# First projection of a two-block transformer kernel: another order of key evictions, pool sums, value-chunk splits and the first query-chunk split

## The reference, cut to what matters

```python
h_x = _modulate(x, g_pre_mix[l], sh1, sc1)      # 256 tokens
h_c = _modulate(ctx, g_pre_mix[l], csh1, csc1)  # 256 context tokens
u_x, q_x, k_x, v_x = _project(h_x, w_in[l])     # 4 x 512 columns
u_c, q_c, k_c, v_c = _project(h_c, w_in[l])     # only k_c and v_c are used
attn_x = _neighbourhood_attention(q_x, k_x, v_x, k_c, v_c, rpb[l])
mix_x = concat([_pool_mixer(u_x, pool_w[l], pool_scale[l]), attn_x]) @ w_out[l]
```

## Time and profile before

| | |
|---|---|
| median of 3 runs | 928.18 us (926.5 to 929.54) |
| profiled execution, its own time | 929.46 us |
| its span in the trace | 927.5 us |
| mean granted TensorE clock | 0.968 of full |
| PE busy | 863.7 us, 93% of the span |
| DVE busy | 521.0 us, 56% |
| ACT busy | 444.2 us, 48% |
| POOL busy | 44.6 us, 5% |
| DMA | 165.87 MB, mean 179 GB/s |

### The profile page before, as it was taken

The page is one execution under the profiler, slowest core; times in us unless marked ns, Lnnn a source line. Parts: engine busy times, 40 slices in busy tenths (PEclk is TensorE's granted clock), DMA queues, the critical chain, the costliest instruction groups (busy, mean ns, idle before and its releaser), DMA issues.

```text
span 927.5 us, 13973 instructions
## 1 busy us (share of the span) xinstructions
PE 863.7 (93%) x5434; PEld 734.9 (79%) x5434; DVE 521.0 (56%) x904; ACT 444.2 (48%) x797; POOL 44.6 (5%) x55
## 2 busy tenths in 40 slices
PE   5898899979999999899999999898798899999996
PEld 3696655749999998679999999785465699999995
DVE  2344167476776565665555554677445565555554
ACT  3553045265545444554444444765445554444442
POOL 1000000000000000000000000055100000000000
PEclk9999799979999999999999999998779999999998
DMA  8966338425787565356555554564012265555521
GB/s 325 397 250 248 116 136 319 159 90 163 262 280 226 182 186 172 102 173 231 182 184 182 196 185 146 207 215 158 0 46 69 92 207 179 194 191 181 185 92 46
DMA packets 45105, 165.87 MB, mean 179 GB/s; under 512 B 4976, under 2 KB 5104, under 8 KB 44784
## 3 DMA queue, kind: packets, MB, share of 16 engines
q1 hardware_dynamic: 45040, 164.98, 51.7%
HBM read 163.91 MB, written 1.05 MB: 178 GB/s over the span
## 4 chain that ended last, share of the span: by engine, by line
PE 83%; DVE 5%; ACT 4%; issue 4%; DMA 2%; POOL 1%; SPq 0%; ACTq 0%; DVEq 0%; POOLq 0%
PE ps L1361 13%; PE ps L1363 13%; PE ps L1362 12%; PE ps L1381 12%; PE ps L1383 12%; PE ps L1385 12%; DMA raw<-in_w_mod_p 2%; PE ps L1608 2%; PE ps L1407 1%; ACT hi L449 1%; DVE lo L866 1%; ACT PT L461 1%; PE ps L1795 1%; PE ps L1801 1%; PE ps L1592 1%
## 5 line engine op out<-in xcount | busy, mean ns | idle before, releaser
L866 DVE TENSOR_TENSOR lo<-raw,hi 128x1024 fp32r<-128x1024 f32 (+1 forms) x247 | 298.9, 1218 | 180.2 <-ACT hi L449 180.0
L449 ACT ACTIVATE hi<-raw 128x1024 fp32r<-128x1024 f32 (+1 forms) x247 | 257.1, 1049 | 78.3 <-PE ps L1385 59.9
L1361 PE MATMUL ps<-Th,hi 128*128 128x256 f32 (+1 forms) x960 | 276.1, 288 | 3.1 <-DVE lo L866 1.7
L1363 PE MATMUL ps<-Th,lo 128*128 128x256 f32 (+1 forms) x960 | 275.0, 287 | 0.0
L1362 PE MATMUL ps<-Tl,hi 128*128 128x256 f32 (+1 forms) x960 | 275.0, 287 | 0.0
L1381 PE MATMUL ps<-hi,Th 128*128 128x512 f32 (+2 forms) x524 | 180.6, 404 | 13.9 <-issue 7.0
L1361 PEld LDWEIGHTS ps<-Th,hi 128*128 128x128 f32 x960 | 184.0, 192 | 8.5 <-issue 3.0
L1362 PEld LDWEIGHTS ps<-Tl,hi 128*128 128x128 f32 x960 | 183.9, 192 | 3.7
L1363 PEld LDWEIGHTS ps<-Th,lo 128*128 128x128 f32 x960 | 183.8, 191 | 1.3
L1383 PE MATMUL ps<-lo,Th 128*128 128x512 f32 (+2 forms) x524 | 175.7, 394 | 0.0
L1385 PE MATMUL ps<-hi,Tl 128*128 128x512 f32 (+2 forms) x524 | 175.4, 394 | 0.0
(11 more groups left out here) (189 smaller groups left out, 622.4 us busy)
## 6 DMA issues: line engine op xcount, KB each, us to landing
raw<-in_ffn_down SPq DMA_DIRECT2D x44, 512.0 KB, 3.6
raw<-in_w_mod_p SPq DMA_DIRECT2D x40, 512.0 KB, 6.1
raw<-in_ffn_gate SPq DMA_DIRECT2D x40, 512.0 KB, 3.2
raw<-in_ffn_up SPq DMA_DIRECT2D x40, 512.0 KB, 3.2
raw<-in_w_mlp_out SPq DMA_DIRECT2D x32, 512.0 KB, 4.5
raw<-in_w_mlp_in SPq DMA_DIRECT2D x28, 512.0 KB, 4.4
raw<-in_w_out SPq DMA_DIRECT2D x16, 512.0 KB, 5.6
raw<-in_w_in_q SPq DMA_DIRECT2D x8, 512.0 KB, 5.7
```

The costliest lines, as they stand in the source:

```text
L449: e.activation(hi[h % RING][:, 0:w], raw[n % RAW][:, 0:w], ACT.Copy).then_inc(s_hi, 1)
L866: e.tensor_tensor(lo[h % RING][:, 0:w], raw[n % RAW][:, 0:w], hi[h % RING][:, 0:w], ALU.subtract).then_inc(s_lo, 1)
L1361: e.matmul(o, a, Th[:, k, c0:c1], start=(k == 0), stop=False)
L1363: return e.matmul(o, b, Th[:, k, c0:c1], start=False, stop=(k == KT - 1))
```

## The change

Three edits, on ACT and DVE alone. The instructions are the same in number and kind; only their order differs. PE, SP and POOL are as before.

1. The split of q0 (`split(4)`) stands ahead of the context's norm on both engines.
2. On ACT, the splits of v0 and v1 stand behind the evictions of k2 and k3, those of v2 and v3 behind `mod_part(0)`. k0 and k1 are evicted right after the split of k3.
3. On DVE, `window(0)` to `window(2)` stand ahead of `lo` of k3 and `window(3)` behind it; then come `lo` of v0 and v1, `mod_part(0)`, and `lo` of v2 and v3.

```diff
@@ ScalarE
                 first_turned(0, j)
+            split(4)
             first_norm(2)
             first_norm(3)
-            split(4)
@@
-            split(CH["w_in_q", 3] + RING)
+            split(CH["w_in_k", 3])
             for a in range(4):
                 h = CH["w_in_k", a]
                 e.wait_ge(s_used, h + 1)
                 e.activation(kT[:, a, 0:512], ps[ROT[a]][:, :], ACT.Copy).then_inc(s_k, 1)
                 e.activation(kT[:, a, 512:672], ps[ROT[a]][:, 0:160], ACT.Copy).then_inc(s_k, 1)
-                split(min(h + RING, CH["w_in_v", 3]))
+                if a >= 2:
+                    split(CH["w_in_v", a - 2])
             mod_part(0)
+            split(CH["w_in_v", 3])
             load_table(ACT.Exp)
@@ VectorE
                 first_low(0, j)
+            split(4)
             first_sum(2)
             first_sum(3)
             first_scaled(2)
             first_scaled(3)
-            split(4)
@@
-            split(CH["w_in_q", 3] + RING)
+            split(CH["w_in_k", 2])
@@
-            for a in range(4):
-                window(a)
-                split(min(CH["w_in_k", a] + RING, CH["w_in_v", 3]))
+            for g in range(3):
+                window(g)
+            split(CH["w_in_k", 3])
+            window(3)
+            split(CH["w_in_v", 1])
             mod_part(0)
+            split(CH["w_in_v", 3])
```

## The result

| | before | changed |
|---|---|---|
| median | 927.51 us (4 runs, 926.5 to 929.54) | 913.58 us (4 runs, 910.07 to 917.61) |
| ratio | | 0.9852, 95% interval 0.9824 to 0.988 |
| profiled execution, its span | 929.46, 927.5 | 917.61, 915.7 |
| mean granted clock in it | 0.968 | 0.973 |

The change is 13.9 us faster where I forecast 11.3; 913.58 lies 0.4 us under the low end of my range, so the range was wrong. (The kernel before has one run more than when I forecast, hence 927.51 and not 928.18.) The interval of the ratio means a gain of 11.1 to 16.3 us and holds the forecast one, so the first question is whether anything is missing from the sum at all.

What follows compares the result with a forecast made beforehand. PE bounds the kernel, losing time only where it stands still or runs slowly, held up by ACT's and DVE's order. 6.96 + 2.37 + 0.35 + 1.66 = 11.34 us takes 928.18 to 916.9; 8-in-10 range 914.0 to 919.9.

Steps and rivals of the forecast that it cites:

- The long wait: PE's wait ahead of the second half of v0, for DVE's late copy of bank 3: 6.96 us, gone in full.
- The evictions of the keys: ACT evicts k0 to k3 ahead of the value splits; in one chain with DVE's reorder, `lo` of v1 starts at 87.15.
- The clock: Second half of v0 and the turn at full clock once the wait goes: 2.37 plus 0.35 us, bounds 0 and 2.72.
- the clock falls anyway: Rival: the clock still falls in v0, or enough wait stays to lower it; gain 8.6 us, 919.6; chance 7%.
- q0's split: PE's wait ahead of q0 on `lo` of q0 goes: 1.66 us saved, bounds 0 and 1.66.
- a late landing takes its place: Rival: moving q0's split pays nothing, as q0 waits for its landing or the transposes for the norm; 918.5, 7%.
- a cover of 1.6 us: Margin of DVE's last context scaling, ending near 46.7, before PE wants it for the transposes at 48.4.
- the 42.8: Landing time of q0's chunk, in us, past which holding the norm behind its DMA was to begin to cost.
- the low end of the range: Lower bound of the 8-in-10 range, 914.0 us, allowing for run spread of 1.5 us and shorter low-clock stretches elsewhere.

Runs made afterwards that it cites:

- dve_order: Only VectorE's order changed (windows 0 to 2 ahead of `lo` of k3, copy ahead of `lo` of v2 and v3) against the kernel before: 918.42 us, ratio 0.9914.
- dve_and_q: The kernel before with VectorE's new order and q0's split ahead of the norm, ScalarE keeping its old order at the keys: 917.45 us, ratio 0.9891.
- q_first: Only the split of q0 moved ahead of the context's norm on both engines, against the kernel before: 926.53 us, ratio 0.9987.
- fill_wait: The kernel before with 27 matmuls that no one reads put into PE's long wait in v0: 923.71 us, ratio 0.997.
- fill_start: The changed kernel with 8 unread matmuls ahead of each of `w_mod` products 9, 10 and 11 in the u stage: 915.58 us, ratio 0.9872.

## Why the prediction was right, and where it was not

**The long wait.** Place and cause were right: all of it is gone, DVE's copy is 0.6 us early. The cause was DVE's order, as I read it from the 0.11 us between its copy and PE's start, and dve_order shows it. The size was a little small: I took the 6.96 us from the modelled end of the last matmul (89.72), but the next one would have started 0.23 us after that matmul's start, at 89.56, so 7.1 us were lost; q0 to v0b shrank by 7.18.

**The evictions of the keys.** I treated ACT's and DVE's edits as one chain and gave neither a price of its own. In fact DVE's is nearly the whole: without ACT's 0.35 us is lost (dve_and_q), and ACT's alone lengthens the wait by 1.3 us.

**The clock.** 2.72 forecast, 2.79 measured alone. The profile of before that I summed from had the dearest such stretch; over the three profiles of before, v0b to v1 averages 6.55 us against 4.43, so the term is worth 2.1 on average. The stage from q0 to the attention gained 10.1 us against the first profile and 9.3 against the mean of three (74.45 to 65.14); forecast 9.68. The forecast lies between them because the two errors of size work against each other. The rival *the clock falls anyway* did not come.

**q0's split.** The 1.66 us are right when its chunk has landed. The rival that a late landing takes its place, against which I counted a cover of 1.6 us, came in part: I watched the norm, but what stood behind the split and was wanted first is the eviction of u, which had only 0.5 us to spare (44.94 against 45.44). So a late landing costs sooner than the 42.8 that I worked out: the one at 41.4 in q_first already did, with PE done with u 0.8 us earlier. In two of eight profiles with this edit PE waited for it, 0.65 and 0.40 us, so the edit is worth 1.5 us on average.

**The step that failed** is the last one of the prediction, the low end of the range: "low end 914.0, for runs of one kernel lie 1.5 us about their median and a low-clock stretch elsewhere, such as that at 202 to 210, may by chance be shorter". That left 2.9 us below the centre for both, and the 1.5 us came from three runs of before. Single executions lie 2.6 to 3.2 us (one standard deviation) about their mean, so a median of four misses by about 2 us as a matter of course (an estimate from that deviation). The miss of 3.3 us at the centre splits into three: I subtracted from 928.18, where 87 executions have a mean of 927.1 (1.1 us); the mean gain is 12.1 and not 11.3 (0.8, within its interval); and the four runs of the result lay low, 913.58 against 915.0 (1.4). The last of these is luck. Whether a mechanism is missing stays open: by the stages the edits are worth 9.3 + 1.5 = 10.8 us on average, 1.3 us less than the 12.1 between the means, which lies within its interval of 1.5. The 1 us from the output projection to the MLP (above) may be part of it.

## What to carry to other kernels

When PE waits for an in-order engine, look at what that engine did before it became busy: here it idled 12 us for a DMA, with 8 us of ready work queued behind that wait. Move ready work ahead of the wait, and count the clock that the idle time costs as well as the idle time. Then check the next instruction behind a moved one, not only the chain you had in mind.

For the range: one profile gives a sum good to a few tenths where the stages repeat, but the time of one execution also holds how long its low-clock stretches happened to be and whether a chunk came late, so the range must be as wide as the spread of executions, not of three runs.

## What the runs showed of the hardware

- Between q0 and the attention the granted clock fell in a wait of 7 to 8 us in every profile that had one (five), and in none of the waits of 1.7 and 1.9 us; matmuls whose result no one reads kept it at 1.00 through the same 7 us. A long wait is not needed for it to fall: in the attention it fell in nine of the fourteen profiles, seven with a wait of 1.0 to 1.7 us there and two (fill_wait, fill_start) in which the longest wait was 0.6 us. The runs do not show what decides it there.
- The low stretches of one and the same kernel are not the same from execution to execution: before q0 those on record lasted 3.4, 10.2 and 6.8 us in three profiles of before, and 10.2, 10.2, 3.4 and 6.8 in four of the changed kernel. PE's work where the clock is full and nothing is waited for repeats to 0.02 us (v1 to attention: 18.30 to 18.32 in all fourteen).
- While the DMAs were at full share (1.02 and 1.01), q0's chunk landed 11.0 us after its issue in the profile of before (29.81 to 40.8) and 10.4 us in q_first (31.01 to 41.4): in q_first it was not the transfer that was slow but its issue that was late, by 1.2 us, while PE ended u 0.8 us earlier. A cover of 0.4 us, read from one execution, was no cover in the next.
